# A fused two-block layer on one core: VectorE's choice pieces cut smaller, the tile counts of one half-block reordered, and the attention heads' work rewritten in another order with three weight buffers

## The reference, cut to what matters

```python
# first layer: choose 16 experts of 128*128 for each token and head
s = einsum('thpd,hpkd->thpk', q, sub_keys)          # 8 heads x 2 halves x 128 keys
top_s, top_i = top_k(s, 16)                          # "choose_halves": 16 lists
cand = top_s[:, :, 0, :, None] + top_s[:, :, 1, None, :]
best_s, best_c = top_k(cand, 16)                     # "choose": 8 lists
gates = softmax(best_s)                              # "chosen_gates"
out = sum_e gate_e * gelu(u_e . x) * v_e             # over all 16384 experts, dense

# second layer, per head (4 heads of each kind, 512 tokens, causal)
z = q k^T / 8; w = exp(log_sigmoid(z) + tail(log_sigmoid(-z)))    # stick-breaking: "sb"
o_sb = w @ v
p = softmax(q1 k1^T + bias) - lam * softmax(q2 k2^T + bias)       # differential: "df"
o_df = rmsnorm(p @ v)
x = x + concat(rg_lru(..) * gelu(ya), o_sb, o_df) @ w_out
```

## Time and profile before

| | |
|---|---|
| three timed runs | 3152.96 us median (3152.2 to 3153.22) |
| the profiled execution | 3152.92 us, span 3151.1 us, mean granted clock 0.992 |
| TensorE | 3072.4 us busy (98%) |
| GpSimd | 2335.3 us busy (74%) |
| VectorE | 1947.7 us busy (62%) |
| ScalarE | 712.3 us busy (23%) |

### The profile page before, as it was taken

One profiled execution on the slowest core, in us unless ns is written; L12 is line 12 of the kernel. 1 busy time (PEld: TensorE's weight loads), 2 busy tenths in 40 slices (PEclk: granted clock), 3 DMA queues, 4 the chain that ended last, 5 costly groups with the idle time before them and its releaser, 6 DMA issues.

```text
span 3151.1 us, 40617 instructions
## 1 busy us (share of the span) xinstructions
PE 3072.4 (98%) x13738; PEld 2474.9 (79%) x13738; DVE 1947.7 (62%) x2787; ACT 712.3 (23%) x1253; POOL 2335.3 (74%) x1127
## 2 busy tenths in 40 slices
PE   8999999999999999999999999999999998899998
PEld 6788777788878878787888888888888775578886
DVE  6488646221254787988876466667767567776621
ACT  3244223220122122121222111111111255332201
POOL 6843654677776889898889888888888762378876
PEclk9999999999999999999999999999999999899999
DMA  4211221233332445444545766666666421123322
GB/s 144 93 48 54 94 72 55 73 100 121 107 94 93 135 176 184 148 159 174 185 175 181 247 188 189 187 192 186 190 188 190 130 75 41 33 88 94 99 93 73
DMA packets 245543, 405.63 MB, mean 129 GB/s; under 512 B 145600, under 2 KB 145728, under 8 KB 244160
## 3 DMA queue, kind: packets, MB, share of 16 engines
q1 hardware_dynamic: 224560, 331.68, 34.0%
q10 hardware_dynamic: 20880, 72.62, 6.0%
HBM read 335.04 MB, written 69.21 MB: 128 GB/s over the span
## 4 chain that ended last, share of the span: by engine, by line
PE 87%; DVE 9%; POOL 1%; issue 1%; ACT 1%; DMA 1%; POOLq 0%; SPq 0%; ACTq 0%; DVEq 0%
PE bank L596 19%; PE bank L598 18%; PE bank L597 18%; PE banks L596 6%; PE banks L598 6%; PE banks L597 6%; PE banks L894 2%; PE banks L745 1%; PE banks L709 1%; PE banks L711 1%; PE banks L710 1%; DVE hot L2293 1%; PE banks L810 1%; DVE gate_stage L2305 1%; DVE hot L2295 1%
## 5 line engine op out<-in xcount | busy, mean ns | idle before, releaser
L503 POOL TENSOR_TENSOR w_hi<-w_raw,ones 128x1024 fp32r<-128x1024 f32 x492 | 956.1, 1943 | 689.5 <-PE bank L598 485.3
L505 POOL TENSOR_TENSOR w_lo<-w_raw,w_hi 128x1024 fp32r<-128x1024 f32 x492 | 1232.3, 2505 | 38.6
L596 PE MATMUL bank<-h_hi,w_hi 128*128 128x512 f32 x2000 | 794.1, 397 | 9.4 <-DVE h_lo L1877 7.1
L598 PE MATMUL bank<-h_hi,w_lo 128*128 128x512 f32 x2000 | 780.6, 390 | 0.0
L597 PE MATMUL bank<-h_lo,w_hi 128*128 128x512 f32 x2000 | 779.8, 390 | 0.0
L596 PEld LDWEIGHTS bank<-h_hi,w_hi 128*128 128x128 f32 x2000 | 377.0, 188 | 93.7 <-DVE h_lo L1877 13.9
L598 PEld LDWEIGHTS bank<-h_hi,w_lo 128*128 128x128 f32 x2000 | 376.2, 188 | 80.8
L597 PEld LDWEIGHTS bank<-h_lo,w_hi 128*128 128x128 f32 x2000 | 376.9, 188 | 75.0 <-issue 2.2
L2365 DVE TENSOR_TENSOR ew_lo<-expert_w,ew_hi 128x512 fp32r<-128x512 f32 x128 | 249.1, 1985 | 181.9 <-ACT ew_hi L1584 178.1
L2361 DVE TENSOR_TENSOR expert_w<-acts_in,gates_in 128x512 f32<-128x512 f32 x128 | 245.3, 1952 | 67.3 <-DMA gates_in<-gates 52.5
L2293 DVE TENSOR_TENSOR hot<-bank,tab 128x512 fp32r<-128x512 f32 x256 | 164.5, 684 | 105.9 <-PE banks L894 105.3
(11 more groups left out here) (443 smaller groups left out, 4579.1 us busy)
## 6 DMA issues: line engine op xcount, KB each, us to landing
w_raw<-weights SPq DMA_DIRECT2D x494, 512.0 KB, 3.6
acts<-act_out_stage ACTq DMA_DIRECT2D x128, 256.0 KB, 2.9
gates<-gate_stage ACTq DMA_DIRECT2D x8, 4096.0 KB, 13.0
acts_in<-acts SPq DMA_DIRECT2D x128, 256.0 KB, 4.3
gates_in<-gates SPq DMA_DIRECT2D x128, 256.0 KB, 4.8
resid<-x SPq DMA_DIRECT2D x4, 512.0 KB, 8.3
resid<-x ACTq DMA_DIRECT2D x4, 512.0 KB, 7.0
out<-final SPq DMA_DIRECT2D x3, 512.0 KB, 2.6
```

The source lines that it names most:

```text
L503: nc.gpsimd.tensor_tensor(w_hi[:, pair, :], w_raw[:, slot, :], one_col.to_broadcast((P, 1024)), ALU.mult).then_inc(hi_split, 1)
L505: nc.gpsimd.tensor_tensor(w_lo[:, pair, :], w_raw[:, slot, :], f32(w_hi[:, pair, :]), ALU.subtract).then_inc(split_done, 1)
L596: mm(out_, hi, rhs_hi, start=first, stop=False)
L598: return mm(out_, lo, rhs_hi, start=False, stop=last)
```

## The change

Three edits of the expert stage and a reordering of the attention stage. The arithmetic is the same.

1. `LOT_TILES`: in lot 6 (steps 48 to 55) the tiles after each step go from 1,1,2,1,1,2,1,2 to 2,1,1,1,2,1,1,2: eleven both times.
2. The 16 lists of `choose_halves` are done in four pieces of 5, 4, 5 and 2 (parts 1, 2, 4, 5) and not three of 7, 7 and 2 (parts 1, 2, 4).
3. What follows moves by one to two parts: `choose` from 5 and 6 to 6 and 7, `places` from 7 to 9, `pick_keys(0)` from 9 to 10, `picked(0)` with `pick_keys(1)` from 10 to 12, `picked(1)` from 12 to 13, where `chosen_gates` stays.
4. `sb_w` gets three places: heads 0 and 2 share the old one, head 1 has one over `mix_hi`'s upper half, head 3 one over `h_hi`. `sb_softplus(h)` now waits only for `sb_out(h-2)`.
5. TensorE's `df_logits(h+1, 0)` and `(h+1, 1)` move ahead of `df_out(h)` and `sb_out(h)`; `out_part`s, `sb_logits(3, ...)` and `df_spread(0)` move with them. VectorE and ScalarE get the matching order; `lru_out` 0 to 3 go later, ScalarE's GELUs of the branch, its squares and root move from the end of a head into the next one, which brings two more table loads.
6. GpSimd's four splits of output weights start on other semaphores.

```diff
-LOT_TILES = ((2, 2, 2, 1, 2, 2, 2, 2), (2, 2, 2, 1, 2, 2, 1, 2)) * 3 + ((1, 1, 2, 1, 1, 2, 1, 2), (2, 1, 1, 2, 1, 1, 1, 1))
+LOT_TILES = ((2, 2, 2, 1, 2, 2, 2, 2), (2, 2, 2, 1, 2, 2, 1, 2)) * 3 + ((2, 1, 1, 1, 2, 1, 1, 2), (2, 1, 1, 2, 1, 1, 1, 1))
...
-    sbw = place("sb_w", [P, TT, T], A0)
+    sbw = [place(name, [P, TT, T], at) for name, at in (("sb_w", A0), ("sb_w1", A0 + 48 * KB))]
+    sbw += [sbw[0], place("sb_w3", [P, TT, T], 32 * KB)]
...
-    MIXED = {0: 1, 1: 2, 2: 3, 6: 4, 3: 5, 7: 6}
+    MIXED = {0: 1, 1: 2, 6: 3, 2: 4, 3: 5, 7: 6}
...
@@ GpSimd
                 pool.wait_ge(sb_z_done, TT * SB_HEADS)
-                pool.wait_ge(mixed_ready, MIXED[3])
+                pool.wait_ge(df_p_ready, TT * 3 + 2)
...
-        pool.wait_ge(mixed_ready, MIXED[1])
+        pool.wait_ge(sb_sp_ready, 3)
         split(0)
+        pool.wait_ge(df_s_done, TT * 3 + 3)
         split(1)
...
@@ TensorE, head 0 (head 1 alike, with the wait for late tile 7)
             df_turn(h, 3)
             filler(h, 11, 12)
+            df_logits(h + 1, 0)
             df_out(h)
+            df_logits(h + 1, 1)
             sb_out(h)
...
@@ TensorE, head 2
         h = 2
-        df_sums(0)
-        pe.wait_ge(acc_read_act, LATE + 8)
-        df_logits(h, 0)
-        out_part(0, 4, True)
-        df_logits(h, 1)
         sb_logits(h + 1, 0)
         sb_logits(h + 1, 1)
+        df_sums(0)
         df_logits(h, 2)
         sb_logits(h + 1, 2)
         sb_logits(h + 1, 3)
-        out_part(0, 0)
         sb_tails(h, 0)
         sb_tails(h, 1)
-        df_spread(0)
         df_turn(h, 0)
         df_logits(h, 3)
+        out_part(0, 4, True)
+        df_spread(0)
+        out_part(0, 0)
         sb_tails(h, 2)
...
@@ VectorE, expert stage
-                if part in (1, 2, 4):
-                    choose_halves(tt + 1, *{1: (0, 7), 2: (7, 14), 4: (14, 16)}[part])
-                elif part == 5:
+                if part in (1, 2, 4, 5):
+                    choose_halves(tt + 1, *{1: (0, 5), 2: (5, 9), 4: (9, 14), 5: (14, 16)}[part])
+                elif part == 6:
                     choose(0, PEER_HEADS // 2)
-                elif part == 6:
+                elif part == 7:
                     choose(PEER_HEADS // 2)
-                elif part == 7:
+                elif part == 9:
                     places(tt + 1)
-                elif part == 9:
+                elif part == 10:
                     pick_keys(tt + 1, 0)
-                elif part == 10:
+                elif part == 12:
                     picked(0)
                     pick_keys(tt + 1, 1)
-                elif part == 12:
+                elif part == 13:
                     picked(1)
-                elif part == 13:
                     chosen_gates()
...
@@ VectorE, attention
-            if h:
-                dve.wait_ge(sb_o_done, h)
+            if h > 1:
+                dve.wait_ge(sb_o_done, h - 1)
...
             df_logits(h, 0)
+            if h:
+                df_logits(h, 1)
             sb_softplus(h)
-            df_logits(h, 1)
+            if h == 0:
+                df_logits(h, 1)
             sb_logs(h)
+            if h == 2:
+                sb_out(0)
```

More of the change, by code:

```diff
@@ L1002, in sb_tails @@
             for j2 in range(j, TT):
-                ins = mm(acc[:, (j2 - j) * P:T - j * P], t_("later") if j2 == j else ones[:], sbw[:, j2, 0:T - j2 * P],
+                ins = mm(acc[:, (j2 - j) * P:T - j * P], t_("later") if j2 == j else ones[:], sbw[h][:, j2, 0:T - j2 * P],
                          start=j2 == j, stop=j2 == TT - 1)
@@ L1143, in _ @@
         df_turn(h, 2)
+        pe.wait_ge(acc_read_act, LATE + 8)
+        df_logits(h + 1, 0)
         df_turn(h, 3)
+        df_logits(h + 1, 1)
         df_out(h)
@@ L1187, in _ @@
         h = 3
-        df_logits(h, 0)
-        out_part(0, 2)
-        df_logits(h, 1)
         out_part(0, 6)
@@ L1196, in _ @@
         df_logits(h, 3)
-        out_part(0, 3)
+        out_part(0, 2)
         sb_tails(h, 2)
@@ L1207, in _ @@
         out_part(1, 2)
+        out_part(0, 3)
         out_part(1, 3)
@@ L1732, in _ @@
         late_tile(2)
+        df_exps(0, 0)
+        late_tile(3)
         for h in range(SB_HEADS):
-            df_exps(h, 0)
-            if h < 2:
-                late_tile(3 + 3 * h)
             df_exps(h, 1)
+            if h == 1:
+                late_tile(6)
+                branch_gelus()
+            if h == 2:
+                df_squares(0)
+                df_root(0)
             if h + 1 < SB_HEADS:
@@ L2469, in sb_logs, with earlier_only @@
                 N = T - j * P
-                tt_(z[:, j, 0:N], z[:, j, 0:N], sbw[:, j, 0:N], ALU.subtract).then_inc(dve_step, 1)
+                tt_(z[:, j, 0:N], z[:, j, 0:N], sbw[h][:, j, 0:N], ALU.subtract).then_inc(dve_step, 1)
             dve.wait_ge(dve_step, c.due(dve_step, TT))
-        def earlier_only(done):
-            tt_(sbw[:, :, 0:P], sbw[:, :, 0:P], t_("earlier").unsqueeze(1).to_broadcast((P, TT, P)), ALU.mult).then_inc(done, 1)
+        def earlier_only(h, done):
+            tt_(sbw[h][:, :, 0:P], sbw[h][:, :, 0:P], t_("earlier").unsqueeze(1).to_broadcast((P, TT, P)), ALU.mult).then_inc(done, 1)
         def sb_tails(h, js):
@@ L2561, in _ @@
                 sb_weights(h)
-                if h == 1:
-                    lru_out(0)
-                    lru_out(1)
             elif h == 2:
                 sb_logits(h + 1, range(TT))
-                earlier_only(sb_sp_ready)
+                earlier_only(h, sb_sp_ready)
                 df_scales(0)
@@ L2570, in _ @@
                 df_maps(h, 0)
-                lru_out(2)
                 sb_tails(h, (0, 1))
@@ L2574, in _ @@
                 df_logits(h, 3)
+                lru_out(0)
                 sb_tails(h, (2, 3))
                 df_maps(h, 2)
+                lru_out(1)
                 df_normed(0)
@@ L2579, in _ @@
                 sb_weights(h)
-                lru_out(3)
             else:
-                earlier_only(sb_sp_ready)
+                earlier_only(h, sb_sp_ready)
+                lru_out(2)
                 df_logits(h, 2)
@@ L2589, in _ @@
                 df_maps(h, 2)
+                lru_out(3)
                 df_maps(h, 3)
@@ L2592, in _ @@
                 rescaled((0, 1, 2, 3))
-            if h % 2:
-                sb_out(h // 2)
+            if h == 3:
+                sb_out(1)
         rescaled((4, 5))
```

25 lines of the change are left out of this document (10 added, 15 removed).

## The result

The changed kernel takes 3124.48 us, median of 4 runs (3123.5 to 3127.1), against 3153.09 us for the kernel before on the same chip (4 runs, 3152.2 to 3153.74). The ratio is 0.9906, 95% interval 0.9895 to 0.9918. That is 28.6 us less where 31.0 were forecast: 2.6 us above the forecast time of 3121.9 and inside the range. A second series on another chip gave 3124.52 (ratio 0.9905, 0.9889 to 0.9922).

The account below looks back on a forecast made before the run. The prediction took TensorE, 87% of the chain, to bound the kernel, with gains only where it stands still. 19.1 + 1.8 + 4.1 + 6 = 31.0 us off 3152.9 gives 3121.9 us; range 3115 to 3131.

Parts of the forecast that it names:

- What bounds it: Whole kernel: TensorE is 87% of the chain; in the expert stage it waits 15.8 us for VectorE's gate sums.
- Edit 2, 19.1 us: Expert steps 3 and 4 of lots 0, 2 and 4: 24.73 us becomes 18.36, 6.37 us three times.
- Edit 3, 1.8 us: Expert steps 11 and 12: moved pieces let the one-hots start earlier, 1.8 us for three, possibly 0.
- start about 1 us earlier: Step 11: with only pick_keys(0) there, VectorE's one-hots start about 1 us earlier, when they are allowed.
- overruns of 0.4 and 0.9 us: VectorE's pieces at parts 5 and 13 exceed a two-tile step's 6.6 us; 1.8 us is covered, price 0.
- Edit 1, 4.1 us: Lot 6: two tiles in step 48 cover the sum's wait for the stored table, 4.1 us.
- Attention, 6 us: Attention heads 2 and 3: 20.6 us of VectorE not at work, less 4.4, 6.7 and 3.5, leaves 6 us.
- the walk: New attention order followed with trace durations at full clock: about 4.4 us of VectorE idle time stays.
- 3.5 on top for the lower clock: Attention: 3.5 us taken off the 9.5 us gain for the lower clock behind TensorE's waits.
- The collisions: Attention: three GpSimd splits hold up VectorE at df_maps, lru_out(2) and df_maps(3, 2), 6.7 us together.
- The rule on VectorE and GpSimd: Attention: by the skill's rule a split could hold VectorE for nearly all its length, not for 2.76 us.
- The first rival: The attention order gives nothing: three splits hold VectorE 4.5 us each, 13.4 us, so 3128 us; chance 0.16.

Follow-up runs that it names:

- e4: The kernel before with choose_halves in pieces of five, four and seven lists at parts 1, 2 and 4, nothing else moved: 3151.58 us, ratio 0.9991.
- b3: The changed kernel with the small choice pieces, but places, pick_keys and picked at their old parts: 3133.2 us, a single run.
- a1: The changed kernel with VectorE's lru_out(0) moved from behind df_logits(2, 3) to between the two pairs of sb_logits(3): 3121.08 us.
- e3: The kernel before with the attention edits alone: 3149.52 us, ratio 0.9982.
- b1: a4 with GpSimd's second split of output weights right behind its first in head 2, in place of head 3: 3120.61 us.
- e1: The kernel before with the smaller and moved choice pieces alone, tile counts and attention as before: 3132.88 us, ratio 0.9927.
- a3: The changed kernel with the first two attention splits cut to 8 of 1024 columns, so the output is not the reference's: 3123.37 us.
- b4: a4 with the first two attention splits cut to 8 of 1024 columns, so part of the projection uses old weights: 3118.64 us.
- a4: a1 with lru_out(1) also moved, to the place lru_out(0) leaves, ahead of the second pair of sb_tails(2): 3119.02 us.

## Why the prediction was right, and where it was off

- **What bounds it.** Right. TensorE's waits of 15.8 us and the lower clock behind them were the cost, and both are gone: 649.95 of 650 us busy at full clock.
- **Edit 2, 19.1 us.** 6.40, 6.33 and 6.29 us in the three blocks, 19.0 in all. Each piece was costed against the room of its own step, and e4 shows that this is how to cost them: the same lists, put together at part 4, give back 15.4 of the 19.0 us in its trace, and by the medians 2.9 us of gain are left.
- **Edit 3, 1.8 us.** Measured 0.44 to 0.47 a block, 1.4 in all. That the one-hots "start about 1 us earlier" was mis-sized: they start 1.04 us into step 11 (1188.31) where it was 1.49 (1193.52), so 0.45 earlier, and that is what the steps gained, not 0.62. The other half of the edit, that `places` must not follow the sum that waits for the table, the prediction did not see (b3: 3.6 us a block). The overruns of 0.4 and 0.9 us were covered, as said.
- **Edit 1, 4.1 us.** Measured 4.2; the distance of steps 48 and 50 is 18.28, forecast 18.4.
- **Attention, 6 us.** Here is the shortfall: 3.6 in the stretch, where 6 was forecast. The term that was mis-sized is the idle time that stays: 4.4 by the walk and 3.5 on top for the lower clock, 7.9, against 11.4 measured. The collisions were put at 6.7 and measured at 5.6. VectorE's waits for ScalarE at the start of heads 2 and 3 came as walked (1.57 and 1.84 us, forecast 1.5 each). The walk had named the other place too (the second pair of `sb_tails(2)`, behind `out_part(0, 0)`, which waits for `lru_out(0)`) at 1.4 us; it is 2.86. Another 1.60 and 1.30 us are waits for TensorE's `sb_logits`, late behind a `df_out(1)` that ran partly at the lower clock, and for its first `sb_tails`, itself at the lower clock. a1 takes TensorE's wait for `lru_out(0)` away, VectorE's wait of 2.86 us falls to 1.14, and it gains 3.4 us by the medians, which shows that this was on the path. It is not the whole cause: e3 has the same order and the same wait of TensorE, and its idle time is 8.6 us, near the 7.9. The other part is where the lower clock fell, for which the forecast had 3.5 us; what sets that place stays open.
- **How firm that size is.** The same attention program took 62.93 and 63.04 us in two executions of one kernel, but 60.33 and 61.91 in two kernels with another expert stage ahead of it (e3, b3), one execution each; the old one took 66.66, 66.63, 65.87 and 68.27. So the stretch gained 3.6 us here and 4.8 on the mean of these, and 6 is at the edge of what an execution gives.
- **The rule on VectorE and GpSimd.** The Trainium skill, SBUF — State Buffer, section "Who interferes with whom", says that whichever of the two engines comes second is blocked for as long as the first's instruction lasts. The trace agrees: the three operations end at 2650.82, 2684.51 and 2691.77, the second halves of the splits at 2650.72, 2684.50 and 2691.75. In the changed kernel it costs at most one such half a split, 2.4 us, since during the first half VectorE was at operations that weren't held up. That is luck of the order: in b1 an operation of 0.35 us took 2.00 beside a first half. The first rival's 4.5 us a split did not come.
- **The rest.** 24.4 and 3.6 us make 28.0; between the expert stage and the stretch 0.9 us were lost, and 0.4 won behind it, which leaves 27.5 in this execution. The medians say 28.6, the forecast 31.0: attention was put 2.4 us too high and the picks 0.4, and the rest is within what executions differ by.

## What to carry to other kernels

Cost work that fills gaps step by step against the room of that very step, and look what else the step has (here a wait for a DMA): the same operations gave 21.6 us (e1) or 2.9 (e4) by the steps they stood in. In a stage in which two engines wait for each other in turns, look for the operation that neither is in need of early and that one is in need of late, as `lru_out(0)`: put it into the idle time just ahead. Durations taken away in such a stage come back in part or not at all (4.2 us gave 2.3 in a3's stretch and nothing that can be seen in b4), so only a run says what they are worth. And look first whether two traces already differ ahead of the edit, as those of a4 and b4 do, before a difference is put down to it.

## What was not expected of the hardware

- The lower clock can fall in another place before two programs differ: a4 and b4 are the same up to the first split of head 2, and in the 6 us from 2632 on TensorE had 1.00 in a4 and 0.52 in b4.
- Two executions of one kernel had the lower clock at the same places to 0.3 us (62.93 and 63.04 us for the stretch), while the same attention order behind another expert stage had a mean of 0.83 in place of 0.78 and took 60.33 us. That kernel was profiled once, so it isn't shown that what ran ahead is the reason.
- Before the change, TensorE's wait of 2.16 us at step 49 (1612.08) was followed by 3.4 us at a granted clock of 0.50, as its waits of 4.28 us were.
- An operation of VectorE on 128x1 elements took 2.29 us beside a split, and 0.16 without one.
